# Reordering how a modulation vector is summed: the two gates first, the second shift and scale later, in a hybrid SSD / gMLP trunk on one core

## The reference, cut to what matters

```python
c_act = jax.nn.silu(c)
mod = (c_act @ ada_w[l] + ada_b[l])[:, None, :]
sh1, sc1, g1, sh2, sc2, g2 = jnp.split(mod, N_MOD, axis=-1)
h = rmsnorm(x, norm1_g[l]) * (1 + sc1) + sh1
x = x + g1 * hybrid_mixer(h, w_in[l], ..., w_out[l])
h = rmsnorm(x, norm2_g[l]) * (1 + sc2) + sh2
x = x + g2 * conv_gated_ffn(h, ff_up[l], ..., ff_down[l])
return rmsnorm(x, final_g)
```

## Time and profile before

| what | value |
|---|---|
| median of three runs | 2803.24 us |
| profiled execution | 2800.92 us |
| its span | 2799.2 us |
| TensorE busy | 2709.3 us (97%) |
| VectorE, ScalarE, GpSimd busy | 1825.6, 994.0, 1046.6 us |
| moved by DMA | 620.49 MB, mean 222 GB/s |

### The profile page before, as it was taken

How to read it: one execution, slowest core, us unless ns; L and a number is a source line. 1 busy time by engine, 2 the same in 40 slices (tenths; PEclk the granted TensorE clock), 3 DMA queues, 4 the chain that set the end, 5 groups by cost and what they waited for, 6 DMA issues and landing times.

```text
span 2799.2 us, 33835 instructions
## 1 busy us (share of the span) xinstructions
PE 2709.3 (97%) x12427; PEld 2214.0 (79%) x12427; DVE 1825.6 (65%) x2598; ACT 994.0 (36%) x1505; POOL 1046.6 (37%) x723
## 2 busy tenths in 40 slices
PE   7999889899999999999999999999999999999998
PEld 6777768677887888877878888888888788887886
DVE  6788765658567666558787667456655855545767
ACT  3544223321143333334444321143223433334333
POOL 2344340455236777744480110001102544444230
PEclk9999999999999999999999999999999999999999
DMA  9677676999955566664447767687676344445656
GB/s 383 235 249 296 221 287 204 335 345 327 317 199 181 192 210 207 200 242 138 159 138 265 256 210 250 204 276 239 220 237 231 104 128 126 127 124 196 220 169 221
DMA packets 262001, 620.49 MB, mean 222 GB/s; under 512 B 26725, under 2 KB 84553, under 8 KB 257739
## 3 DMA queue, kind: packets, MB, share of 16 engines
q1 hardware_dynamic: 261174, 618.08, 64.6%
q10 hardware_dynamic: 662, 0.24, 0.0%
HBM read 466.57 MB, written 151.66 MB: 221 GB/s over the span
## 4 chain that ended last, share of the span: by engine, by line
PE 76%; DVE 8%; DMA 6%; issue 3%; POOL 2%; SPq 2%; ACT 1%; DVEq 0%; ACTq 0%; POOLq 0%
PE main L1984 29%; PE pair L2254 15%; PE main L2254 14%; PE pair L2274 6%; PE main L2274 5%; DMA w_split_scratch<-w_hl 2%; PE pair L2121 2%; DMA t_up_scratch<-tb 1%; POOL w_hl L717 1%; PE pair L2146 1%; POOL tb L728 1%; DVE a_lo L1605 1%; DMA tb<-in_ff_up_dram 1%; PE pair L2106 1%; PE pair L2113 1%
## 5 line engine op out<-in xcount | busy, mean ns | idle before, releaser
L717 POOL TENSOR_TENSOR w_hl<-w_raw,w_hl 128x512 fp32r<-128x512 f32 x532 | 760.6, 1434 | 915.1 <-ACT w_hl L817 902.4
L817 ACT ACTIVATE w_hl<-w_raw 128x512 fp32r<-128x512 f32 x532 | 332.6, 630 | 830.9 <-PE main L2254 168.4
L1984 PE MATMUL main<-w_hl,h_hi 128*128 128x512 f32 x1536 | 491.3, 401 | 9.6 <-DMA w_hl<-w_split_scratch 7.2
L1984 PEld LDWEIGHTS main<-w_hl,h_hi 128*128 128x128 f32 x1536 | 283.7, 188 | 84.1 <-issue 16.6
L1984 PE MATMUL main<-w_hl,h_lo 128*128 128x512 f32 x768 | 300.2, 391 | 0.0
L728 POOL TENSOR_TENSOR tb<-tb,tb 128x512 f32<-128x512 f32 x132 | 201.3, 1525 | 184.1 <-DMA tb<-in_ff_up_dram 179.4
L754 POOL TENSOR_TENSOR pre_hl<-pre_raw,pre_hl 128x512 fp32r<-128x512 f32 x35 | 53.4, 1528 | 563.8 <-ACT pre_hl L841 563.8
L1984 PE MATMUL main<-h_hi,w_hl 128*128 128x512 f32 x768 | 250.8, 401 | 6.6 <-ACT stage L896 5.0
L2254 PE MATMUL pair<-s_hi,w_hl 128*128 128x512 f32 x736 | 235.7, 393 | 2.3 <-POOL w_hl L717 2.3
L2274 PE MATMUL main<-w_hl,a_hi 128*128 128x512 f32 x704 | 219.0, 392 | 7.6 <-DVE a_lo L1605 4.0
L1605 DVE TENSOR_TENSOR a_lo<-g,a_hi 128x512 fp32r<-128x512 f32 x132 | 160.2, 1222 | 97.7 <-ACT a_hi L1067 97.1
(11 more groups left out here) (287 smaller groups left out, 5079.8 us busy)
## 6 DMA issues: line engine op xcount, KB each, us to landing
w_hl<-w_split_scratch SPq DMA_DIRECT2D x312, 512.0 KB, 4.4
w_split_scratch<-w_hl SPq DMA_DIRECT2D x104, 512.0 KB, 6.7
w_raw<-t_up_scratch SPq DMA_DIRECT2D x176, 256.0 KB, 2.7
w_raw<-in_ff_up_dram SPq DMA_DIRECT2D x132, 256.0 KB, 3.7
tb<-in_ff_up_dram SPq DMA_DIRECT2D x88, 256.0 KB, 4.2
t_up_scratch<-tb SPq DMA_DIRECT2D x88, 256.0 KB, 5.6
g_scratch<-c_val SPq DMA_DIRECT2D x44, 512.0 KB, 4.0
g<-g_scratch SPq DMA_DIRECT2D x40, 512.0 KB, 7.3
```

The costliest lines, as they stand in the source:

```text
L717: nc.gpsimd.tensor_tensor(w_lo[:, g % RING, :], w_raw[:, g % RING, :], w_hi[:, g % RING, :].bitcast(F32), ALU.subtract).then_inc(w_lo_ok, 1)
L817: nc.scalar.activation(w_hi[:, g % RING, :], w_raw[:, g % RING, :], ACT.Copy).then_inc(w_hi_ok, 1)
L1984: ins = T.matmul(main[i], a, w, start=first and p == 0, stop=last and p == 2)
```

## The change

The order of the two late products is swapped. Ring tiles 8 to 15 now hold the two gates (pieces 2 and 5 of each row, one strided transfer of 1 MB). Tiles 8 to 11 stay ahead of the load of unit 4. Tiles 12 to 15 are loaded ahead of units 8, 11, 14 and 17. VectorE sums four tiles during product A, one behind `dt_first`, one behind `dt_rest`, two behind the ws products. The four gate matmuls stand behind unit 23 and wait for these sums, and the gate bias rows are loaded at unit 20. Chunk scores 0 wait for the gate row. Shift and scale of the second norm come as eight tiles of 128 x 2048 (`col_load`) ahead of units 20 (tile 1, into a buffer of its own), 28, 40, 48, 56, 68, 78, 84; `col_sum` stands at the old places of `gate_sums` except where the diff shows another. Their 16 matmuls stand behind unit 83, their columns behind `norm_x`, and the x2 loads ahead of unit 89 wait for them.

```diff
-        ADA_RING, ADA_FIRST, HF0, ADA_PE = 12, 4, 2, 2
+        ADA_RING, ADA_FIRST, HF0, ADA_PE = 12, 8, 2, 2
-        gate_rows, _ = fixed("gate_rows", [1, 2 * D], F32, r_at + 80 * KB)
+        gate_rows, _ = fixed("gate_rows", [1, 2 * D], F32, x2_at)
+        col_spare, _ = fixed("col_spare", [P, 2 * D], F32, r_at + 48 * KB)
-        GATE_AT = (22, 34, 42, 50, 58, 70, 80, 85)
+        GATE_TILES = {8: 12, 11: 13, 14: 14, 17: 15}
+        COL_AT = {20: 1, 28: 0, 40: 2, 48: 3, 56: 4, 68: 5, 78: 6, 84: 7}
...
             for i in range(ADA_RING, 2 * KD):
                 xbc_unit(0, i - ADA_RING + RING)
-                ada_load(i)
...
+            def col_load(k):
+                if k == 0:
+                    sp.wait_ge(gate_mm, 4)
+                elif k == 1:
+                    sp.wait_ge(ada_summed, KD + 3 - ADA_PE)
+                else:
+                    sp.wait_ge(ada_summed, GATES_SUMMED + k)
+                src = ada_w[0, k * P:(k + 1) * P, 3 * D:5 * D]
...
+                if b == 0 and n in GATE_TILES:
+                    ada_load(GATE_TILES[n])
+                if b == 0 and n in COL_AT:
+                    col_load(COL_AT[n])
+                if b == 0 and n == 20:
...
+                if b == 0 and n == 30:
                     sp.wait_ge(gate_ok, 4)
...
                     if n == x2_at_unit:
                         if b == 0:
-                            sp.wait_ge(gate_mm, 4)
+                            sp.wait_ge(mod_col, 4)
...
-            for i in range(KD, KD + 5):
+            for i in range(KD, KD + 4):
                 ada_sum(i)
...
                         dt_first()
-                        for i in range(KD + 5, 2 * KD):
-                            ada_sum(i)
+                        ada_sum(KD + 4)
...
                         dt_rest()
+                        ada_sum(KD + 5)
...
+                    if b == 0 and j == 1:
+                        ada_sum(KD + 6)
+                        ada_sum(KD + 7)
+                        dve.wait_ge(bias_in, 32)
+                        for m in range(4):
+                            dve.wait_ge(gate_mm, m + 1)
+                            row = gate_rows[0:1, m * W:(m + 1) * W]
+                            V.tensor_tensor(row, aux[m][0:1, :], row, ALU.add).then_inc(gate_ok, 1)
...
-                    if b == 0 and j == 2:
-                        gate_sums(0)
...
                     if b == 0 and cc < NT - 1:
-                        gate_sums(cc + 1)
+                        if cc == 0:
+                            col_sum(0)
+                        col_sum(cc + 1)
...
+                if b == 0:
+                    col_sum(5)
                 gate_y(1)
...
-                    gate_sums(5)
+                    col_sum(6)
...
-                    gate_sums(6)
+                    col_sum(7)
...
-                        if b == 0 and (j, k) == (2, 2):
-                            pe.wait_ge(ada_summed, 2 * KD - ADA_PE)
-                            mod_column(1, range(KD), aux[0])
+                        if b == 0 and (j, k) == (2, 7):
+                            pe.wait_ge(ada_summed, GATES_SUMMED)
+                            pe.wait_ge(ws_ok, 2)
+                            pe.wait_ge(acs_t_ok, 1)
+                            for m in range(4):
+                                T.matmul(aux[m][0:1, :], ones, mod_sum[:, 2 + m // 2, (m % 2) * W:(m % 2 + 1) * W],
+                                         start=True, stop=True).then_inc(gate_mm, 1)
...
-                        pe.wait_ge(ready, 3)
+                        pe.wait_ge(gate_ok, 4)
...
-                        if b == 0 and j == 0 and k == 15:
+                        if b == 0 and j == 0 and k == 11:
                             pe.wait_ge(y_lo_ok, KD)
-                            pe.wait_ge(ada_summed, 4 * KD - ADA_PE)
...
+                            pe.wait_ge(ada_summed, GATES_SUMMED + KD)
+                            mod_column(range(KD), aux[0])
```

More of the change, by code:

```diff
@@ L413, in ada_load @@
             def ada_load(i):
-                part, k = (0, 3)[i // KD], i % KD
+                k = i % KD
                 if i >= ADA_RING:
                     sp.wait_ge(mod_col, 2)
-                sp.dma_start(ada_t[:, (i + ADA_FIRST) % ADA_RING, :],
-                             ada_w[0, k * P:(k + 1) * P, part * D:(part + 2) * D]).then_inc(ada_in[i % ADA_RING], 16)
+                rows_k = ada_w[0, k * P:(k + 1) * P, :]
+                if i < KD:
+                    src = rows_k[:, 0:2 * D].rearrange("p (m d) -> p m d", m=2)
+                else:
+                    src = rows_k.rearrange("p (h m d) -> p h m d", h=2, m=3)[:, :, 2, :]
+                sp.dma_start(ada_t[:, (i + ADA_FIRST) % ADA_RING, :].rearrange("p (m d) -> p m d", m=2), src
+                             ).then_inc(ada_in[i % ADA_RING], 16)
             sp.dma_start(c_rows[:], c[0].rearrange("(k p) -> k p", p=P)).then_inc(c_in, 16)
@@ L433, in _ @@
                 xbc_unit(0, i - ADA_RING + RING)
-                ada_load(i)
             sp.dma_start(ws_raw[:], gm_ws[0].rearrange("h t s -> t h s")).then_inc(pro_dma, 16)
[L437 to L444, removed]
+            def col_load(k):
[3 more added lines that the diff above has]
+                    sp.wait_ge(ada_summed, KD + 3 - ADA_PE)
+                else:
+                    sp.wait_ge(ada_summed, GATES_SUMMED + k)
+                src = ada_w[0, k * P:(k + 1) * P, 3 * D:5 * D]
+                if k == 1:
+                    sp.dma_start(col_spare[:], src).then_inc(ada_in[5], 16)
+                else:
+                    sp.dma_start(mod_sum[:, 2:4, :].rearrange("p m d -> p (m d)"), src).then_inc(ada_in[4 + k % 2], 16)
             def k_pair(dst):
@@ L1269, in _ @@
                     h_lows(0, (0, 1), aux, full_at)
-            for i in range(KD, KD + 5):
+            for i in range(KD, KD + 4):
                 ada_sum(i)
[L1272 to L1275, removed]
+                k = i - KD + 4
+                dve.wait_ge(h_lo_ok, k)
+                h_lows(0, (k,), aux, full_at)
             dve.wait_ge(wdt_h, 1)
@@ L1568, in mixer @@
                 if b == 0:
-                    gate_sums(7)
-                    dve.wait_ge(pro_dma, 48)
-                    for m in range(4):
-                        dve.wait_ge(gate_mm, m + 1)
-                        row = gate_rows[0:1, m * W:(m + 1) * W]
-                        V.tensor_tensor(row, aux[m][0:1, :], row, ALU.add).then_inc(gate_ok, 1)
+                    mod_columns(1, slice(0, KD), aux[0], two_parts(col_b, R_AB + 2 * KD, slice(0, KD)), R_N2, 3)
                 if b == 0:
@@ L1934, in _, with mod_column @@
             ones = tri[:, P - 1:P]
-            def mod_column(n, ks, bank):
+            def mod_column(ks, bank):
                 for k in ks:
@@ L1940, in mod_column @@
                         m = part * KD + k
-                        last = T.matmul(bank[:, m:m + 1], mod_sum[:, 2 * n + part, k * P:(k + 1) * P], ones,
+                        last = T.matmul(bank[:, m:m + 1], mod_sum[:, part, k * P:(k + 1) * P], ones,
                                         start=True, stop=True)
@@ L1965, in _ @@
             pe.wait_ge(ada_summed, KD - ADA_PE)
-            mod_column(0, range(4), main[3])
-            mod_column(0, range(4, KD), main[2])
+            mod_column(range(4), main[3])
+            mod_column(range(4, KD), main[2])
             def weights_in(b, n):
```

43 lines of the change are left out of this document (17 added, 26 removed).

## The result

The changed kernel takes 2782.93 us, median of four runs (2778.50 to 2785.73), against 2802.15 us for the kernel before (2801.02 to 2805.23): 19.2 us less, a ratio of 0.9928 with a 95% interval of 0.9911 to 0.9945. The forecast was 2774, 29 us less. The profiled execution has a span of 2780.8 us, 18.4 less.

A forecast was written before the change was run, and what follows sets the result against it. TensorE, busy 2709.3 of 2799.2 us, was taken as the bound, its waits as the prize. 10.2 - 0.5 - 2.5 - 0.4 + 12.1 + 9.9 = 28.8, so 2803.24 - 29 = 2774 us; own range 2769 to 2779, 8 in 10 within 2764 to 2790.

The forecast's parts named there:

- four large waits: TensorE's waits before unit 8 (5.02 us), dt*a transposes (2.78), amid y transposes (10.31), before the output projection's right half (7.87).
- rival A: SyncE's holds still reach TensorE in part: 3 us at unit 28, 6 in the output projection; 2783 us, chance 0.17.
- Part 1: Start, units 4 to 11: moving four ada_w tiles removes the 5.02 us wait and 2.0 us slow clock; gain 7.0 us.
- Part 2: Product B: dt*a wait gone, new 3.4 us wait before gate matmuls; gain 10.2 us so far, the start's included.
- the 2.78 us wait: TensorE's wait before the dt*a transposes, behind three VectorE sums; forecast gone, with 3.1 us of slow clock.
- Part 3: SyncE held at unit 28 for the gate matmuls: no wait, nothing to spare; copies for first yoff late, -0.5 us.
- Part 4: Other column tiles: -2.5 us from the tile ahead of unit 56, -0.4 us from tile 5's sum before gate_y(1).
- Part 5: Output projection: the 10.31 and 7.87 us waits go with their slow clock, +12.1 and +9.9 us.
- The sum: All terms together 28.8, say 29 us, with mixer 1 onward taken as the same work behind in-order TensorE.

The follow-up runs named there:

- experiment 6: Changed kernel with gate sum 13 moved from behind the dt chain to behind the ws products, together with sums 14 and 15; 2784.31 us.
- experiment 7: Kernel of experiment 5 with the splits of units 19 and 20 written ahead of product B's first SiLU tile; 2779.76 us against 2802.48.
- experiment 12: Kernel of experiment 11 with the splits of units 19 to 22 all written ahead of product B's first SiLU tile; 2773.89 us against 2802.49.
- experiment 4: Changed kernel with the shift and scale column matmuls behind unit 87 instead of behind unit 83; 2790.97 us.
- experiment 5: Changed kernel with column tile 4 loaded ahead of unit 58 instead of 56; 2778.67 us against 2804.01.
- experiment 10: Changed kernel itself, unedited, measured and profiled again; 2781.39 us against 2802.48.
- experiment 3: Changed kernel with the sum of column tile 5 behind y_ok instead of ahead of gate_y(1); 2792.12 us.
- experiment 1: Kernel before with one edit: ring tiles 12 to 15 loaded ahead of units 8, 11, 14 and 17; 2796.75 us against 2803.28.
- experiment 11: Kernel of experiment 7 with gate matmuls behind unit 25, row additions between product C's convs, SyncE's hold at unit 34; 2774.90 us against 2802.48.
- experiment 8: Kernel before with 132 GpSimd sums of weight quarters cut from 512 to 8 columns (timing only, not the layer); 2792.83 us.
- experiment 9: Changed kernel with the same 132 GpSimd sums cut to 8 columns (timing only, not the layer); 2771.16 us.

## Why the prediction was right, and where it was off

- **Sign and range: right, the number in part by luck.** All four large waits named as removed are gone, and 2782.93 lies inside 2764 to 2790, outside the forecast's own range of 2769 to 2779. It is rival A's 2783, but A had put 6 of its 9 us on the holds of SyncE in the output projection, which cost nothing there. The gain is two thirds of the forecast 29 us, and half of what is missing was lost where the sum had no term.
- **Part 1: right.** 7.0 us forecast; 6.5 us alone in time, 7.6 in the trace; undone, the lead at mixer 1 falls by 6.8.
- **Part 2: the removed waits right, the new one in the wrong place.** I had 3.4 us at the gate matmuls; it is 1.81 there and 4.06 at unit 19. The step that failed is "The columns move away and four gate matmuls, 3.59 us, come in behind unit 23: even." The columns' 4.84 us were the cover of split 19, which stands behind a SiLU tile and so behind VectorE. With them gone TensorE arrived first, waited 4.06 us and ran on at 0.50. Experiments 6, 7 and 12 show the chain behind the wait; that the columns were its cover is argued from the order of the work, no run puts them back. Lead 8.1 instead of 10.2 us. The same kernel up to this place has 8.1, 8.8, 9.1 and 9.9 us in experiments 4, 5, 10 and 3, so the error is 0.3 to 2.1 us.
- **The slow clock of product B may not have been the wait's.** The forecast charged 3.1 us of it to the 2.78 us wait. But the clock was 1.00 from 108.36 to 113.70 in before and fell within the columns, and in the changed kernel it fell behind the same 32 matmuls with no wait near. Nine of the ten profiles with these matmuls behind unit 83 and no wait beside them show 3.4 or 6.8 us at 0.50 there (not experiment 3). So the columns seem to bring slow clock with them, 1.7 us for 3.4 us at half rate, and the move took it to the output projection. No run has the 2.78 us wait without the columns. In experiment 12 a wait of 3.09 us without them was followed by 0.50 as well (108.94 to 112.00), so both may count.
- **Part 3: right in its doubt, too small.** No wait at unit 28; from the first scores to chunk 1 the lead falls by 1.3 us instead of 0.5, behind the wait before the first yoff. In the other profiles with the hold at unit 28 it falls by 1.5 to 3.9 us, in experiments 1, 11 and 12, without that hold, by 0.1 at most. Experiment 11 moved the gate matmuls together with the hold.
- **Part 4: right, slightly small.** 2.5 us forecast for tile 4, 3.0 measured, and its cause shown by experiment 5. I put the loss at the gMLP transposes' wait, "up from 1.1 to some 3.6"; it stayed 1.12 and the loss showed ahead of it, 1.35 us at the spatial matmuls and in the units' start. For tile 5's sum I had 0.4; the lead fell by 1.4, and the y transposes waited 1.26 us where none over 1 us was forecast. The sum took the forecast 2.34 us, but the y scaling behind it took 4.29 instead of 3.26; in experiment 3, without the sum ahead of it, it took 3.26 again.
- **Part 5: right.** 22.0 forecast, 21.8 measured. SyncE's hold at unit 78 ended at 316.38, ahead of the 319.7 of the forecast; experiments 3 and 4 each bring back their wait.
- **The sum: one term was missing.** "Mixer 1 onward is the same work behind one in-order TensorE" is true of TensorE's instructions and not of the time. Mixer 1 gave back 4.7 us, most of it where VectorE's work takes longer beside GpSimd's (experiments 8 and 9). I had weighed the two engines against each other for the two gate sums only.

## What to carry to other kernels

Before moving work off the in-order engine that bounds a kernel, ask which late thing it had been covering: list what each queue has behind a wait at that place, and count the moved work as its cover. A transfer that waits for a sum must be placed by when the sum ends, and its place in the queue of loads is worth the time of everything issued behind it. A stage with no edit can still change its time where two engines slow each other, so a gain should be read at checkpoints, not at the end alone. And a single pair of operations that met badly proves little: add up all that met, in both kernels.

## What the runs showed of the hardware

- After a wait of 4.06 us the granted clock was 0.50 in the next 3.13 us and 0.75 in the 4 us behind; after 4.02 us at the same unit in experiment 10 it was 0.71 and 0.80; after 1.81 us it was 1.00. After 5.08 us (experiment 6) the four gate matmuls took 5.91 instead of 3.59 us.
- The clock also falls while TensorE has no idle time: behind 32 matmuls of one column (351.55 to 355.18, at 1.00) it was 0.50 for 3.40 us.
- The same four VectorE operations took 2.49 or 5.57 us, the latter beside four 128 x 512 operations of GpSimd, 6.05 us. With 132 of those cut to 8 columns, the kernel before ran 11.2 us faster (2792.83 against 2804.01), though GpSimd was busy 37% of the span. GpSimd is held up too: beside VectorE's three sums of 10.00 us its low parts of units 17 and 18 took 2.62 and 3.20 us in before, the two ahead of them 1.29 and 1.28.
- From the end of a hold of SyncE to the next split of ScalarE it took 8.2 us in the changed kernel (316.38 to 324.59), 8.1 in experiment 3 (331.48 to 339.55) and 10.5 in before.
